# Value matmuls of one attention branch moved two units later, and a join that waits on their bank

## The reference, cut to what matters

```python
h = rms_norm(x, norm_mix[l])
z = h @ w_in[l]                       # 1024 x 6656
qa, ka, va, qb, kb, vb, uc, gz = jnp.split(z, SPLIT_POINTS, axis=-1)
# A: 8 query heads, 2 key/value heads of 64; dense softmax attention
qa = rope(rms_norm(qa)); ka = rope(rms_norm(ka))
ya = dense_gqa(qa, ka, va) @ w_branch_a[l]
# B: 12 heads of 64, dilated windows; the same steps with a mask
yb = windowed(qb, kb, vb) @ w_branch_b[l]
# C: pooled means, a 128 x 128 map per group, a scale per channel
yc = multiscale_pool(uc, pool_lin[l], pool_scale[l]) @ w_branch_c[l]
g = sigmoid(gz + b_gate[l])
x = x + (g0 * ya + g1 * yb + g2 * yc) @ w_out[l]
x = x + (silu(h2 @ w_ffn_gate[l]) * (h2 @ w_ffn_up[l])) @ w_ffn_down[l]
```

## Time and profile before

| | us |
|---|---|
| median of 3 runs | 810.91 (810.03 to 812.22) |
| the profiled execution | 810.14 |
| its span in the trace | 808.3 |
| PE busy in the span | 802.1 |
| DVE busy | 572.9 |
| ACT busy | 464.0 |
| POOL busy | 245.9 |

### The profile page before, as it was taken

The page is one execution under the profiler, slowest core; times in us unless marked ns, Lnnn a source line. Parts: engine busy times, 40 slices in busy tenths (PEclk is TensorE's granted clock), DMA queues, the critical chain, the costliest instruction groups (busy, mean ns, idle before and its releaser), DMA issues.

```text
span 808.3 us, 9803 instructions
## 1 busy us (share of the span) xinstructions
PE 802.1 (99%) x3808; PEld 658.5 (81%) x3808; DVE 572.9 (71%) x684; ACT 464.0 (57%) x534; POOL 245.9 (30%) x206
## 2 busy tenths in 40 slices
PE   8999999999999999999999999999999999999998
PEld 6888877888888888888888887878888888888886
DVE  5899976758685666665379998777686666676551
ACT  5788886574355445544457888856635455355420
POOL 1342623330043444430023325342300444344200
PEclk9999999999999999999999999999999999999999
DMA  9788876864557787686456888675744666776651
GB/s 336 285 242 217 216 225 216 215 223 161 171 211 210 212 220 218 202 244 217 163 203 201 223 226 215 214 222 190 234 156 167 222 207 208 231 234 201 206 205 53
DMA packets 98318, 170.22 MB, mean 211 GB/s; under 512 B 78016, under 2 KB 78176, under 8 KB 80864
## 3 DMA queue, kind: packets, MB, share of 16 engines
q1 hardware_dynamic: 96352, 163.34, 65.5%
q0 software_dynamic: 1632, 6.18, 2.2%
q10 hardware_dynamic: 288, 0.08, 0.0%
HBM read 149.91 MB, written 1.05 MB: 187 GB/s over the span
## 4 chain that ended last, share of the span: by engine, by line
PE 97%; DVE 1%; DMA 1%; ACT 0%; SPq 0%; issue 0%
PE bank L1135 31%; PE bank L1146 30%; PE bank L1137 30%; PE bank L1257 2%; PE bank L1168 1%; PE bank L1234 1%; PE bank L1225 1%; PE bank L1195 1%; DMA x_sb<-in_x_dram 1%; PE bank L1201 0%; DVE w_lo L854 0%; DVE w_lo L860 0%; ACT w_hi L658 0%; DVE scratch L878 0%; DVE aT_lo L887 0%; ACT aT_hi L670 0%
## 5 line engine op out<-in xcount | busy, mean ns | idle before, releaser
L854 DVE TENSOR_TENSOR w_lo<-w_raw,w_hi 128x2048 fp32r<-128x2048 f32 x134 | 314.6, 2349 | 122.5 <-ACT w_hi L658 121.9
L658 ACT ACTIVATE w_hi<-w_raw 128x2048 fp32r<-128x2048 f32 x134 | 256.5, 1915 | 170.3 <-DMA w_raw<-in_stream_dram 170.3
L1135 PE MATMUL bank<-w_hi,aT_hi 128*128 128x512 f32 x832 | 327.6, 394 | 0.2 <-issue 0.2
L1137 PE MATMUL bank<-w_hi,aT_lo 128*128 128x512 f32 x832 | 324.1, 390 | 0.0
L1146 PE MATMUL bank<-w_lo,aT_hi 128*128 128x512 f32 x832 | 223.3, 390 | 0.2 <-DVE w_lo L854 0.2
L1135 PEld LDWEIGHTS bank<-w_hi,aT_hi 128*128 128x128 f32 x832 | 156.2, 188 | 36.6 <-issue 3.4
L1146 PEld LDWEIGHTS bank<-w_lo,aT_hi 128*128 128x128 f32 x832 | 155.6, 188 | 33.0 <-DVE w_lo L854 0.7
L1137 PEld LDWEIGHTS bank<-w_hi,aT_lo 128*128 128x128 f32 x832 | 156.3, 188 | 31.9
L597 POOL COPY halves<-hid 128x512 uint16<-128x512 uint16 x44 | 75.1, 1734 | 4.6 <-DVE hid L1107 4.6
L606 POOL COPY hT_raw<-turned 128x512 uint16<-128x512 uint16 x44 | 33.8, 813 | 134.4 <-DMA turned<-halves 134.4
L1135 PE MATMUL bank<-w_hi,hT_hi 128*128 128x512 f32 x176 | 68.6, 390 | 0.0
(11 more groups left out here) (102 smaller groups left out, 801.6 us busy)
## 6 DMA issues: line engine op xcount, KB each, us to landing
w_raw<-in_stream_dram SPq DMA_DIRECT2D x135, 1024.0 KB, 5.2
bias_sb<-in_b_gate_dram POOLq DMA_DIRECT2D x12, 256.0 KB, 5.7
par<-in_params_dram POOLq DMA_DIRECT2D x3, 384.0 KB, 3.4
w_raw<-in_stream_dram SPq DMA_DIRECT2D x4, 256.0 KB, 5.0
pool_mat<-in_pooling_dram POOLq DMA_DIRECT2D x1, 1024.0 KB, 5.2
out_dram<-x_sb SPq DMA_DIRECT2D x4, 256.0 KB, 3.9
x_sb<-in_x_dram SPq DMA_DIRECT2D x2, 256.0 KB, 4.6
x_sb<-in_x_dram SPq DMA_DIRECT2D x1, 512.0 KB, 7.0
```

The lines of the kernel that those rows point to most:

```text
L658: nc.scalar.activation(w_hi[:, j % RING, :, :].rearrange("p k n -> p (k n)"), w_raw[:, j % RING, :, :].rearrange("p k n -> p (k n)"), ACT. ...
L854: nc.vector.tensor_tensor(w[0], w[1], w[2].bitcast(F32), ALU.subtract).then_inc(unit_lo, 1)
L1135: nc.tensor.matmul(o, src[0][:, k, tok], w_hi[:, slot, wk + i, :], start=first and i == 0, stop=False)
L1137: nc.tensor.matmul(o, src[1][:, k, tok], w_hi[:, slot, wk + i, :], start=False, stop=False)
```

## The change

Two pairs of value matmuls of branch A go from units 16 and 20 to units 18 and 22, where they follow the score matmuls of that unit at once; those of B stay in units 24 and 28. `TURNS_WITHIN` moves what reads them: ("o", 0) from 17 to 19, ("o", 1) from 20 to 22; and the `mixed` matmuls go from units 21 and 23 to units 19 and 21. One `mixed` tile moves from bank 3 to bank 2. A join from pair 2 on now waits for the signal that the value tile before is full, instead of for a finished unit. No instruction is added or removed.

```diff
-    14: [("pool", 0)], 16: [("pool", 1)], 17: [("o", 0)], 20: [("o", 1)], 21: [("mixed", 0)], 23: [("mixed", 1)],
+    14: [("pool", 0)], 16: [("pool", 1)], 19: [("o", 0), ("mixed", 0)], 21: [("mixed", 1)], 22: [("o", 1)],
...
+def values_at(t):
+
+    return {18: 0, 22: 1, 24: 2, 28: 3}.get(t)
...
-    order[2] += [("o", 0), ("o", 2)]
-    order[3] += [("pool", 0), ("pool", 1), ("o", 1), ("mixed", 0), ("mixed", 1), ("o", 3)]
+    order[2] += [("o", 0), ("mixed", 1), ("o", 2)]
+    order[3] += [("pool", 0), ("pool", 1), ("mixed", 0), ("o", 1), ("o", 3)]
...
                 if i >= 4:
-                    pool.wait_ge(unit_done, lay * UNITS + RING + t)
+                    wait_full(pool, lay, ("o", i // 4 - 1))
...
-                    q = quad_at(t, 6)
+                    q = values_at(t)
                     if q is not None:
                         values(lay, 2 * q)
                         values(lay, 2 * q + 1)
```

## The result

The changed kernel takes **843.3 us** (median of 6 runs, 839.7 to 845.3), the kernel before 810.5 (6 runs): a ratio of 1.039, 95% interval 1.037 to 1.041. It is slower, as forecast, but by 33 us instead of 20, and 2 us above the upper end of the range, 841.

What follows compares the result with a forecast made beforehand. PE bounds the kernel, busy 99% of the span. Stalls of 17.4 us, less 0.8 saved, plus 3.0 for the clock give +19.6 on 810.1, 829.7; with 0.8 for the median, 830.5 us, range 820 to 841.

Steps and rivals of the forecast that it cites:

- part 4: After PE's long stall at unit 20 the clock falls: 1.5 us each, 3.0 for two layers, ends 0 and 6.
- part 3: Late loads of units 21 and 25 make PE stand 6.1 us at unit 20 and 2.6 at unit 24.
- parts 2 and 3: Late joins send SP's load of unit 21 out 8.1 us later, so DVE frees z10's bank late and PE stands.
- +4.1, +7.5 and +8.8: Predicted us after unit 18's start: joins start, second copy ends, load of unit 21 goes out.
- Landing 6.1, high end 7.0: From issue of unit 21's load until ACT can start on it, 6.1 us; high end 7.0, as for unit 25.
- What else is late and costs nothing: Pair 5's second transposition, loads 22 to 24 and later joins were claimed not to hold PE.
- The 2.6 us one near the short idle: PE's stall at unit 24, likened to a 1.01 us idle that kept the upper clock; no fall priced there.
- 3.0 us more: If the clock also fell at the second stall, unit 24: 3.0 us more, 833.5 in all.
- The saving: Direct change from row to column tiles at four moved places saves 0.2 us each, 0.8 in all; ends 0 and 1.4.
- the way in and out: Switches around the value matmuls on PE: 0.25 us or a bit more, 0.35 counting the slow first pair.
- The high end by the same sum: Stalls of 8.3 and 4.8 us in each of two layers plus 6 for the clock: +32, 843.

## Why the prediction was right and wrong

The mechanism was right, and its sizes were not: of the 12.7 us missing, 5.5 are the clock (part 4), 4.7 the stalls, mainly the landing of the late loads (part 3), and 2.5 a wait that the prediction put at nothing.

- *The chain* (parts 2 and 3) was right at each link up to the issue of the load, +4.1, +7.5 and +8.8, and so was PE's arrival at unit 20, +15.9 against +15.8. Undoing a link at SP or at the buffer took 30 us away.
- *The landing* was mis-sized. "Landing 6.1, high end 7.0": it is 6.8 to 7.8 in the change, and 5.2 to 5.7 once the bias load is moved. The surplus over 6.1, summed over the four loads, is 4.2 us, most of the 4.7 us by which the stalls exceed the sum. In the change POOL issues a bias load 1.4 us ahead of each late weight load, because the late joins hold both; the prediction moved the weight load in time and did not ask what would now stand beside it. In the kernel before, the bias loads go out 0.6 to 1.4 us behind those weight loads, which land after 6.1, 7.0, 5.7 and 5.2 us. Why unit 25 took 7.0 there stays open.
- *"What else is late and costs nothing"* put at nothing a cover that was there. The values of unit 16 hid the read of z7, as those of unit 20 hid that of z9. I asked this for unit 20 alone. It cost 2.5 us, about what the time lies above the range; the row that shows it was in the trace of before.
- *The clock* (part 4) was priced at one fall a layer of 1.5 us; it fell at all four long stalls, for 8.5 us together, 2.1 each. "The 2.6 us one near the short idle" was the wrong side to choose, and with 3.9 and 4.7 us it was not that short. The rule of the Trainium skill, TensorE: Matmul & The Clock Gate, section on the HAM clock gate, weighed there as 3.0 us more, was nearer.
- *The saving* was 0.2 a place as taken: 0.20 by the rows above, 0.21 with the next few matmuls, 0.9 us in all. Of the 0.35 that the way in and out was put at, 0.15 is left: a direct change of tiling mode still costs something, as one expects by the Trainium skill's TensorEngine Tiling (Array Packing), Key Properties (a change of mode drains). That this rest is a drain is not shown.
- *The range.* The high end by the same sum was 843, and I cut it to 841. The three misses add (4.7 + 5.5 + 2.5 = 12.7 us, from 830.5 to 843.2): they are not independent, since a longer stall also brings the lower clock.

## What to carry to other kernels

Before a producer is moved later on the engine that bounds, follow its signal through every queue in which something waits for it, and ask what else is in that queue: here a weight load stood behind a transposition that stood behind a copy. Ask of every place that loses work which late read that work was hiding, by comparing when the bank is free with when the engine would come without it. And price a new stall with the slower clock behind it: here that made the 22 us of the long stalls into 31.

## What the runs showed of the hardware that was not expected

A 256 KB broadcast load from GpSimd's queue 1.4 us ahead of a 1 MB load made that one land 6.8 to 7.8 us after its issue, instead of 5.2 to 5.7 with the small load 2.8 us behind it; another 1 MB load right behind it hardly mattered (6.7 to 7.1 with it held back). It is not the only thing that does so: in the kernel with the bias loads later, one load at 504.83 took 7.0 us with no bias load within 10 us of it. The lower clock followed idle stretches of PE of 2.5 us (once), 2.7 (twice) and all longer ones, and, the start-up aside, none of those of 2.0 us or less in these runs; how the clock decides is not shown. A call of matmul on plain float32 operands ran as two matmuls in the trace (45 calls, 90 rows). A row tile followed at once by column tiles costs 4.02 us where the two apart cost 4.22.
